# A two-layer hybrid decoder trunk: another way into the mixer, another order around the delta-rule keys, and an S5 pair one level earlier

## What is computed

```python
D_MODEL, SEQ, DEPTH, D_FF, N_BRANCH = 1024, 256, 2, 2816, 4

def rms_norm(x, w, eps=NORM_EPS):
    return x * lax.rsqrt(jnp.mean(x * x, axis=-1, keepdims=True) + eps) * w

for l in range(DEPTH):
    x = x + 0.5 * swiglu(rms_norm(x, ffn1_norm[l]), ffn1_w_gate[l], ffn1_w_up[l], ffn1_w_down[l])
    x = x + hybrid_mixer(rms_norm(x, mix_norm[l]), ...)
    x = x + 0.5 * swiglu(rms_norm(x, ffn2_norm[l]), ffn2_w_gate[l], ffn2_w_up[l], ffn2_w_down[l])
return rms_norm(x, final_norm)

def hybrid_mixer(hn, ...):
    proj = hn @ w_in            # qkv, z, beta, a, s5 u, lru x, lru y, ret q k v g, 4 x 1024 gate logits
    out_a = gated_deltanet(...) # chunks of 64: kk = k k^T, triangular_solve, then a scan over chunks
    out_b = s5_layer(...)       # bu = B u; x_t = abar x_(t-1) + bu_t (complex); y = C x + D u; gelu, glu
    out_c = rg_lru_block(...)   # "griffin": conv, gates, linear recurrence, times gelu(y)
    out_d = retention(...)
    gates = jax.nn.sigmoid(gate_logits.reshape(b, s, N_BRANCH, D_MODEL))
    merged = jnp.sum(gates * jnp.einsum("bsnc,ncd->bsnd", branches, w_branch), axis=2)
    return merged @ w_out
```

## Time and profile before

| | |
|---|---|
| median of 3 runs | 1349.58 us (1348.81 to 1350.08) |
| the profiled execution | 1352.41 us, of which span 1349.9 us |
| mean granted TensorE clock | 0.988 of full |
| PE busy | 1308.1 us, 97% of the span, 11728 matmuls |
| PE idle | 41.8 us (span less busy) |
| DVE, ACT, POOL busy | 931.2, 660.2, 230.4 us |
| DMA | 220.24 MB, 163 GB/s in the mean, weights 50.4% of 16 queues' time |

### The profile page before, as it was taken

One profiled execution on the slowest core, in us unless ns is written; L12 is line 12 of the kernel. 1 busy time (PEld: TensorE's weight loads), 2 busy tenths in 40 slices (PEclk: granted clock), 3 DMA queues, 4 the chain that ended last, 5 costly groups with the idle time before them and its releaser, 6 DMA issues. The chain is left out here.

```text
span 1349.9 us, 27445 instructions
## 1 busy us (share of the span) xinstructions
PE 1308.1 (97%) x11728; PEld 1272.2 (94%) x11728; DVE 931.2 (69%) x1435; ACT 660.2 (49%) x953; POOL 230.4 (17%) x183
## 2 busy tenths in 40 slices
PE   8999999989999999999999999999889999999997
PEld 8999999988788999999999999999877899999997
DVE  5788675875966866666657885567678578566654
ACT  6544647642234464444454455477322355544442
POOL 1000011004733610000100000200157254100000
PEclk9999999989999999999999999999999999999999
DMA  5655664533232555666646556454422335555562
GB/s 200 234 185 188 199 195 127 185 123 126 64 126 74 178 179 196 188 196 221 193 144 201 180 176 214 151 174 148 147 82 78 126 112 192 166 188 187 182 206 97
DMA packets 61465, 220.24 MB, mean 163 GB/s; under 512 B 6944, under 2 KB 7200, under 8 KB 60960
## 3 DMA queue, kind: packets, MB, share of 16 engines
q1 hardware_dynamic: 61344, 218.50, 50.4%
HBM read 217.42 MB, written 1.05 MB: 162 GB/s over the span
## 5 line engine op out<-in xcount | busy, mean ns | idle before, releaser
L447 PE MATMUL bank<-xh,whi 128*128 128x256 f32 x2256 | 642.4, 285 | 8.8 <-DVE wlo L1303 7.0
L448 PE MATMUL bank<-xl,whi 128*128 128x256 f32 x2256 | 633.9, 281 | 0.0
L449 PE MATMUL bank<-xh,wlo 128*128 128x256 f32 x2256 | 633.3, 281 | 0.0
L1303 DVE TENSOR_TENSOR wlo<-raw,whi 128x1024 fp32r<-128x1024 f32 (+1 forms) x384 | 469.2, 1244 | 228.9 <-ACT whi L905 227.2
L905 ACT ACTIVATE whi<-raw 128x1024 fp32r<-128x1024 f32 (+1 forms) x414 | 419.6, 1035 | 175.1 <-DMA raw<-weights 91.1
L447 PEld LDWEIGHTS bank<-xh,whi 128*128 128x128 f32 x2256 | 428.3, 190 | 16.2 <-issue 8.0
L448 PEld LDWEIGHTS bank<-xl,whi 128*128 128x128 f32 x2256 | 428.5, 190 | 0.2
L449 PEld LDWEIGHTS bank<-xh,wlo 128*128 128x128 f32 x2256 | 428.1, 190 | 0.0
L447 PE MATMUL bank<-hh,whi 128*128 128x256 f32 x704 | 196.9, 280 | 0.0
L449 PE MATMUL bank<-hh,wlo 128*128 128x256 f32 x704 | 196.8, 280 | 0.0
L448 PE MATMUL bank<-hl,whi 128*128 128x256 f32 x704 | 196.3, 279 | 0.0
(11 more groups left out here) (366 smaller groups left out, 1444.9 us busy)
## 6 DMA issues: line engine op xcount, KB each, us to landing
raw<-weights SPq DMA_DIRECT2D x350, 512.0 KB, 4.1
raw<-weights SPq DMA_DIRECT2D x64, 448.0 KB, 4.0
cst<-consts SPq DMA_DIRECT2D x1, 1088.0 KB, 8.2
par<-params SPq DMA_DIRECT2D x1, 1072.5 KB, 9.2
par<-params SPq DMA_DIRECT2D x1, 1060.5 KB, 8.3
x<-x_in SPq DMA_DIRECT2D x2, 512.0 KB, 7.4
y_out<-ret SPq DMA_DIRECT2D x4, 256.0 KB, 2.3
ropec<-positions SPq DMA_DIRECT2D x1, 128.0 KB, 8.4
```

Source lines behind the costliest of these rows:

```text
L447: mm(out, w[0], a[0], start=start, stop=False)
L448: mm(out, w[0], a[1], start=False, stop=False)
L449: return mm(out, w[1], a[0], start=False, stop=stop)
L1303: V.tensor_tensor(slot(wlo, i), slot(raw, i), r32(slot(whi, i)), ALU.subtract).then_inc(S("low_dve"), 1)
```

## The change

**Into the mixer.** A new pair of tiles `xrh`, `xrl` holds x times the norm weights, split; it is made while `dn1` ends, tile by tile, as x is complete (ACT `high_scaled`, DVE `low_scaled`). The sums go in the middle of `first_two` for `ba` and `qkv0`, the spreading of the inverse a little later (into two banks at once). `ba`, `qkv0` and `qkv1` run on `xrh` and `xrl`, and DVE multiplies by the inverse when it evicts them. The normed x is made as before, now for `qkv2` and all behind it. The idle matmuls are gone there.

**Banks.** Main has three, side four.

**Keys first.** DVE evicts `ktr`, `vtr`, `gb0`, `gb1` and does `griffin` and `qdec` after them.

**S5.** `s5_in(0)` and `s5_in(1)` run before gate `g2`, and level lv runs the inputs and states 2lv+2 and 2lv+3. The outputs stay where they were.

```diff
+LATE_PROJ = ["ba", "qkv0", "qkv1"]
-        + [("invm", "dve")] + [(n, "act") for n in PROJ] + [(f"g{i}", "act") for i in range(16)]
+        + [(n, "dve" if n in LATE_PROJ else "act") for n in PROJ] + [(f"g{i}", "act") for i in range(16)]
...
-        + [(n, "dve") for n in ("gb0", "gb1", "kk0", "bb0", "kk1", "bb1", "qk0", "qk1")]
+        + [(n, "dve") for n in ("gb0", "gb1", "kk0", "bb0", "kk1", "bb1", "pq0", "pq1", "qk0", "qk1")]
...
+        xrh, xrl = two("xrh", KD, dt=F32R, over="ret"), two("xrl", KD, dt=F32R, over="qkv")
-        main = Units(MAIN, psum[0:4])
-        side = Units(SIDE, psum[4:7])
+        main = Units(MAIN, psum[0:3])
+        side = Units(SIDE, psum[3:7])
-        inv_bank = psum[5]
+        inv_bank, norm_bank = psum[5], psum[4]
...
-            ffn(1, 0)
-            keep_busy(3)
-            pe.wait_ge(*since("inv_rms", 1))
-            inverse_norms("m")
-            first_two(["ba", "qkv0"], norm_tile, 7)
-            for unit in PROJ[2:8]:
+            ffn(1, None)
+            first_two(["ba", "qkv0"], lambda k: since("scaled", KD + k + 1), 0,
+                      early={5: lambda: late_sums(0)}, late={2: lambda: late_inverse("m")})
+            pair("qkv1")
+            half("qkv2", 0, {k: lambda k=k: pe.wait_ge(*norm_tile(k)) for k in range(KD)})
+            half("qkv2", 1)
+            for unit in PROJ[4:8]:
...
+            pe.wait_ge(S("main_act"), main.taken("su"))
+            s5_in(0)
+            s5_in(1)
             gate(2)
             against_k("qk0", 0, 0)
             against_k("qk1", 0, 1)
             gate(3)
...
-                if lv < 4:
-                    s5_in(2 * lv)
-                    s5_in(2 * lv + 1)
+                if lv < 3:
+                    s5_in(2 * lv + 2)
+                    s5_in(2 * lv + 3)
                 if 0 < lv < 5:
                     s5_out(2 * lv - 2)
                     s5_out(2 * lv - 1)
...
@@ ACT @@
             rms(0)
-            high_inputs("m")
+            split_to(split[0] + 1)
+            copy_inverse(2)
+            high_inputs()
             split_to(piece_at("qkv1.0") + 1)
-            act.wait_ge(S("main"), main.ready("ba"))
-            A(tmpB[:, 0, :], main.bank("ba")[:, 0:SEQ], ACT.Identity, bias=par_("dtb")).then_inc(S("main_act"), 1)
+            act.wait_ge(S("main_dve"), main.taken("ba"))
+            link(A(tmpB[:, 0, :], tmpB[:, 0, :], ACT.Identity, bias=par_("dtb")))
...
@@ DVE @@
-            down("dn1_", 0.5, between=None if Now.layer else rope_turns)
+            down("dn1_", 0.5, low=lambda ks: low_scaled("m", "nm", ks), between=None if Now.layer else rope_turns)
+            split_to(piece_at("qkv1.0") + 1)
             inverted(0)
-            normed("m", "nm")
-            split_to(piece_at("qkv1.1") + 1)
+            normed("nm", 2)
+            dve.wait_ge(*since("inv_copied", 2))
+            dve.wait_ge(S("main"), main.ready("ba"))
+            V.tensor_tensor(tmpB[:, 0, :], main.bank("ba")[:, 0:SEQ], invb, ALU.mult).then_inc(S("main_dve"), 1)
             split_to(piece_at("qkv2.0") + 1)
+            late_evicted(0)
+            split_to(piece_at("qkv2.1") + 1)
+            late_evicted(1)
...
-            ahead("g2")
-            for hp in range(2):
-                dve.wait_ge(S("side"), side.ready(f"qk{hp}"))
-                V.tensor_tensor(flat(attn)[:, hp, :], side.bank(f"qk{hp}")[:, 0:256], ...)
+            ahead("g2")
             dve.wait_ge(S("tables"), 2)
+            s5_state(0)
+            for hp in range(2):
+                dve.wait_ge(S("side"), side.ready(f"qk{hp}"))
+                V.tensor_tensor(flat(attn)[:, hp, :], side.bank(f"qk{hp}")[:, 0:256], ...)
             ahead("g3")
+            s5_state(1)
```

More of the change, by code:

```diff
@@ L481, in sum_of_last @@
                 last.then_inc(S("sums"), 1)
-            def inverse_norms(norm):
-                ps = main_bank(f"inv{norm}")
-                for j in range(2):
-                    last = mm(ps[:, j * P:(j + 1) * P], inv_rms[:, j:j + 1].to_broadcast([P, P]), ident, start=True, stop=True)
-                last.then_inc(S("main"), 1)
             def half(unit, o, at={}):
@@ L498, in half @@
                     high, low = mgh, mgl
+                elif unit in LATE_PROJ:
+                    high, low = xrh, xrl
                 else:
@@ L544, in first_two @@
             def first_two(units, arrived, wait, bank=4, early={}, mid={}, late={}):
-                high, low = (mgh, mgl) if units[0] == "wo0" else (xh, xl)
+                high, low = {"wo0": (mgh, mgl), "ba": (xrh, xrl)}.get(units[0], (xh, xl))
                 banks = [main_bank(u) for u in units]
@@ L923, in squares @@
                     act.wait_ge(S("main_dve"), main.taken(unit))
+                    if which == 0:
+                        high_scaled(xrh, "nm", range(tiles.start, tiles.stop))
                     if which == 1:
-                        high_scaled("n2", range(tiles.start, tiles.stop))
+                        high_scaled(xh, "n2", range(tiles.start, tiles.stop))
                     if which == 2 and Now.layer + 1 < DEPTH:
@@ L928, in squares @@
                         act.wait_ge(S("par"), 16)
-                        high_scaled("n1", range(tiles.start, tiles.stop))
+                        high_scaled(xh, "n1", range(tiles.start, tiles.stop))
                         Now.layer -= 1
@@ L1052, in first_taps @@
             def first_taps(i):
-                act.wait_ge(S("main_act"), main.taken(f"qkv{i}"))
+                if i < 2:
+                    act.wait_ge(S("main_dve"), main.taken(f"qkv{i}"))
+                    act.wait_ge(S("main"), main.ready("qkv1"))
+                else:
+                    act.wait_ge(S("main_act"), main.taken(f"qkv{i}"))
                 for t in (2 * i, 2 * i + 1):
@@ L1059, in scalar_layer @@
                 ahead(f"qkv{i}")
[L1060 to L1061 removed]
+                if i == 2:
+                    act.wait_ge(S("main"), main.ready(f"qkv{i}"))
+                    A(qkvp[:, 2 * i:2 * i + 2, 3:], halves(main.bank(f"qkv{i}")[:]), ACT.Identity).then_inc(S("main_act"), 1)
                 if i:
@@ L1142, in scalar_layer @@
             gate(1)
+            act.wait_ge(S("griffin"), 1)
+            A(brh[:, 2], griffin, ACT.Copy).then_inc(S("branch_high"), 1)
             gate(2)
@@ L1323, in inverted, with normed @@
                 V.reciprocal(inv_rms, rms_col).then_inc(S("inv_rms"), 1)
-            def normed(norm, wname):
-                dve.wait_ge(S("main"), main.ready(f"inv{norm}"))
-                ps = main.bank(f"inv{norm}")
+            def normed(wname, n):
+                dve.wait_ge(*since("inverse", n))
                 for k in range(KD):
-                    last = V.scalar_tensor_tensor(flat8[:, k, :], x[:, k, :], par_(wname, k, k + 1), ps[:, 0:SEQ], ALU.mult, ALU.mult)
-                    last.then_inc(*((S("xf"), 1) if k < KD - 1 else (S("main_dve"), 1)))
+                    if k == 4:
+                        split_to(piece_at("qkv1.1") + 1)
+                    V.scalar_tensor_tensor(flat8[:, k, :], x[:, k, :], par_(wname, k, k + 1), norm_bank[:, 0:SEQ], ALU.mult, ALU.mult).then_inc(S("xf"), 1)
                     if k >= 2:
@@ L1668, in vector_layer @@
                 last.then_inc(S("side_dve"), 1)
+            dve.wait_ge(S("gelu_t"), 1)
+            link(V.scalar_tensor_tensor(tmpD, tmpD, 1.0, ly, ALU.add, ALU.mult))
+            V.scalar_tensor_tensor(griffin, tmpF, 0.5, tmpD, ALU.mult, ALU.mult).then_inc(S("griffin"), 1)
+            dve.wait_ge(S("side_act"), side.taken("eb"))
+            V.tensor_tensor(qdec, qkv[:, 0:2, :], egb, ALU.mult).then_inc(S("dve_q"), 1)
+            ahead("g1")
             tj = lambda m, hp: m[:, hp].rearrange("p t j c -> p (t j) c")
```

81 lines of the change are left out of this document (38 added, 43 removed).

## The result

The changed kernel takes **1340.22 us** (median of 7 runs, 1335.51 to 1343.61) against 1350.08 us before in the same comparison (7 runs, 1348.81 to 1352.17): a ratio of 0.9926, with a 95% interval of 0.9908 to 0.9943. It is faster, by 9.9 us, where 25.6 were forecast, and it lies above the range, which ended at 1338. It also spreads over 8 us where the kernel before spreads over 3. The profiled execution took 1339.08 us, span 1337.3.

What follows compares the result with a forecast made beforehand. PE, busy 97% of the span, was taken as the bound, so order could win only its waits, idle matmuls and lost clock. 0 + 7.8 + 2 x 8.9 = 25.6 us, median 1349.6 to 1324; range 1312 to 1338.

Steps and rivals of the forecast that it cites:

- the price of the clock: Anywhere on PE: a wait of over 2 us costs 1.65 us of clock, one of 1.3 us or less nothing.
- Rival C: Mixer: some six short waits a layer, three of them costing 1.65 us of clock each; 1334 us, chance 18%.
- Part 1, the entry: Into the mixer: 4.4 us a layer raw gain, given back by a 2.7 us wait at lx.0 and its clock; 0.
- Part 2, the banks: Three main banks and four side banks: 0, with a bound of 1 us a layer in loss.
- Part 3, keys first: Key evictions: the wait of gb1 and its half clock go; 4.6 us in layer 0, 3.2 in layer 1.
- Part 4, the lead: Levels, S5 inputs a level ahead: 65.4 us less 54.3 and 2.2 of remaining waits, 8.9 us a layer won.
- "1.6" for the pair: At the keys: s5_in(0) and s5_in(1) added there cost 1.6 us where the two do not overlap.
- "0.8" for the wait: At the keys: the wait for kk0's eviction, for the bank of pq0, put at 0.8 us.
- "PEclk at 1.00 from the keys to the end of the levels": Sign in the profile after: full clock over that stretch, where dips would mean that short waits cost the clock.
- The "12.8 us" of the loop: Levels: outputs, POOL's way back, scans, split, eviction and pair sum to 12.8 us, against 11.6 that PE has.
- D: Levels: POOL's place in the loop is unchanged, waits come back elsewhere and only the keys gain; 1342 us, chance 14%.
- S: Levels: POOL's ways back slow beside DVE's splits, 20.6 us of waits a layer instead of 2.2; 1361 us, chance 5%.

Runs made afterwards that it cites:

- `pq1` in step: The changed kernel with s5_in(1) moved behind qk1, and pq1 behind qk1 in the table of side units: 1335.04 us, ratio to before 0.9895.
- the entry with `lx.0` mended: Entry, banks and keys as changed, no S5 lead, with the splits of lx.0 on ACT and DVE put ahead of the tanh: 1331.39 us, ratio 0.9861.
- the lead in step on the old entry: Kernel before with banks, keys and S5 lead, ordered g2, s5_in(0), qk0, qk1, s5_in(1), g3, without the new entry: 1331.48 us, ratio 0.9861.

## Why the prediction was wrong

- **What bounds the kernel, and the price of the clock: a step that failed.** That order could win time only in PE's waits held. "Nothing for one of 1.3 us or less" did not: in layer 0 of the changed kernel the clock fell to 0.50 behind a wait of 0.28 us, 2.6 us lost in `g2`, and in layer 1, where the longest wait at that place was 0.6 us, it did not fall. Behind the wait at `lx.0` it fell in layer 1 and not in layer 0. The trace of before had the answer, in a row that the prediction did not take in; PE behind the levels, and the window after it:

```profile
410.70 0.71 PE L788 MATMUL bank<-big,qkvp 64*128 64x128 f32 x4 [1.28 <-DVE big L1752]
```

```profile
412.10:415.50 3.40, 3.40 (x20) 2.84 (x17) 1.19 (x3) 0.60 (x1) 1.78 (x1) 0.51 0.71 270
```

  Layer 1 has the same there, 1.30 us and 0.51. With the banks alone the same wait of 1.30 us stands in both layers, and the clock does not fall behind it. So the length of the wait did not set the price, and the row of level 2 with 1.30 us and 1.00 showed one outcome of two. Rival C (short waits cost the clock too) was right about this. It was weighed with the Trainium skill, "TensorE: Matmul & The Clock Gate", section "A second HAM failure mode: psum-queue depth-cycling", by which frequent tiny pauses of PE between groups can make the clock swing; this case's trace agrees in layer 0 (0.28 us) and not in layer 1 (0.6 us). A size was off as well: 5.00 us with 25 products lost 2.1 us, and not 2.5.
- **Part 1, the entry: right in its mechanism, and in its number by sizes that cancel.** 0 was forecast; alone it measures 0.9998 (0.9986 to 1.0011). The wait at `lx.0` was 2.30 for 2.7, behind the chain that was named, and all but went when the split went ahead of it. But the raw gain was 3.0 us and not 4.4 (from the last product of `dn1` to where PE was ready for `lx`, 22.4 us for 25.5), and the clock fell behind the wait in one layer only. Not seen: up to 2 us given back in layer 1 at `g0`.
- **Part 2, the banks: the step that failed by most, upward.** "I take 0" stands beside a sentence saying that the fourth bank takes away the wait by itself; the sum then gave the wait to part 3. Banks alone are worth 18.4 us. Of them 11.7 are the keys (29.6 and 28.4 to 23.3 and 23.0), 3 the clock behind `u`, and 3.9 the levels; cut the other way, some 10 are the clock, by the estimate above.
- **Part 3, keys first: wrong about its cause, and it adds nothing.** Before the cost of the pair, the sum had 7.0 and 5.6 us for both layers; the runs show 6.9 and 5.7. But banks and keys, 1332.2, are no better than banks alone, 1331.7. Keys alone are worth 13 us: two remedies for one wait.
- **Part 4, the lead: the step that failed downward.** "8.9 us a layer" was for the levels. They fell by 3.8 and 3.2 us against the kernel before, and by 2.5 and 3.2 against the same kernel without the lead. Terms of two places were mis-sized.

  At the keys, "1.6" for the pair and "0.8" for the wait were 7.3 and 4.5, of which 3.3 and 1.7 went with `pq1` in step, most of it the wait on a count whose table and list disagree (in layer 0 the stretch at the lower clock got shorter too). I had read DVE's new order, with state 1 behind the `qk` evictions, and the new table, with `pq1` ahead of `qk0`, and had not laid them side by side.

  In the levels the waits were not what was wrong: 2.2 us were forecast, each under 1.3, and PE idled 2.4 and 3.0 us, none over 0.8. What was put at nothing is the clock: "PEclk at 1.00 from the keys to the end of the levels" was 0.94 in both layers, some 3 us in each by the estimate above. In layer 0 that is 3 of the 5.1 us between the 54.5 forecast up to the rotation and the 59.6 measured; another 1.0 is that the outputs of level 4 still come singly behind POOL (2.0 us for 1.0). Over the whole kernel the lead costs 0.003 of mean clock (0.989 for 0.992, and 0.989 still with `pq1` in step), 4 us by the same estimate. The "12.8 us" of the loop from POOL to the outputs measured 13.3 (331.69 to 345.01). But a whole turn of level 2 took 15.4 (331.46 to 346.87): the sum left out the outputs themselves, 1.0 us at full clock and 1.9 here at 0.50, though POOL cannot begin before the last of them:

```profile
331.69 1.29 POOL L1249 TENSOR_TENSOR tmpE<-tmpC,wide 128x512 f32<-128x512 f32 x1 [5.73 <-PE bank L718]
```

```profile
341.02 1.15 PE L747 MATMUL bank<-big 64*64 64x64 f32 x32 [0.75 <-DVE tmpD L1710]
342.10 0.69 PE L700 MATMUL bank<-su,par 32*128 32x256 f32 x2
...
343.59 0.69 PE L700 MATMUL bank<-su,par 32*128 32x256 f32 x2 [0.36 <-DVE big L1729]
```

  The second fence is PE in level 2 of the changed kernel: `xy` waits for the scan that frees the bank of `pq5`, and the second input, 1.5 us after the first, for the split and the eviction that the sum had.
- **The rivals.** D, that the lead is eaten, came nearest, with 1342, but by two wrongs, which is luck: its keys gain was 7.8 where the banks gave 18.4, and the lead lost 5.7 instead of nothing. C was near too, with 1334, and had the mechanism of the levels. S did not come: in the changed kernel POOL's first operations took 1.29 and 1.26 us for states 2 and 3 of layer 0, no longer 2.1 (state 6 took 2.35).

The parts as measured, in the order in which they were put together: banks and keys -17.1 us, the entry on top +2.3, the lead on top +5.7; of this last, 5.2 went with `pq1` in step.

The fastest kernels that compute the whole are the banks alone (1331.7), the entry with `lx.0` mended (1331.4) and the lead in step on the old entry (1331.5), which these runs can't tell apart. The first is two lines.

## What to carry to other kernels

When a wait is for a bank, price the bank before the order: one more bank in the ring took the whole wait, and reordering the evictions on top of it took nothing that these runs can tell. Where waits are counts over a table, a reordering is right only if the table's order and the engine's list move together; lay the two side by side for each unit moved, since a wrong count can show as nothing but a wait. A loop through several engines is to be summed all the way round, with the outputs that free its buffers too. And read all the waits of one length, with the granted clock behind each, before giving waits of that length a price.
